# Two kinds of softmax attention in a transformer block kernel: normalising the numerators on GpSimd, and turning them over later

## The reference, cut to what matters

```python
scores = jnp.einsum('bqkgd,bskd->bkgqs', qb, k) * scale
p = jax.nn.softmax(scores, axis=-1)
o = jnp.einsum('bkgqs,bskd->bqkgd', p, v)
y_attn = o * jax.nn.silu(g_a)          # second block only
```

## Time and profile before

| | us |
|---|---|
| median of 3 runs (lowest, highest) | 3885.12 (3881.82, 3887.04) |
| the profiled execution: its time, its span | 3889.09, 3887.3 |
| busy in the span: TensorE, VectorE, ScalarE, GpSimd | 3536.8, 1918.4, 1351.0, 149.0 |
| mean granted TensorE clock | 0.951 of full |
| masked attention, first to last exp | 1330.1 to 1534.7 |
| unmasked attentions, first to last exp | 2790.4 to 2998.5, and one at 3528.7 to 3736.8 |

### The profile page before, as it was taken

The page is one execution under the profiler, slowest core; times in us unless marked ns, Lnnn a source line. Parts: engine busy times, 40 slices in busy tenths (PEclk is TensorE's granted clock), DMA queues, the critical chain, the costliest instruction groups (busy, mean ns, idle before and its releaser), DMA issues.

```text
span 3887.3 us, 41660 instructions
## 1 busy us (share of the span) xinstructions
PE 3536.8 (91%) x17310; PEld 2888.9 (74%) x17310; DVE 1918.4 (49%) x2459; ACT 1351.0 (35%) x1874; POOL 149.0 (4%) x261
## 2 busy tenths in 40 slices
PE   5999999988987698899999998889898988998987
PEld 3888888866975587778888885678887745887875
DVE  6233333366427698353333335622588365137964
ACT  4111111154222388221111113521487064126843
POOL 0000000000100110000000000010100001000000
PEclk8999999999996799999999999999999989999998
DMA  5222221213741453122222221231611103243111
GB/s 194 89 83 71 82 92 66 76 66 98 184 168 39 82 87 61 44 87 71 90 72 78 76 76 38 77 111 60 180 28 33 49 23 102 85 131 98 28 39 44
DMA packets 146619, 316.58 MB, mean 81 GB/s; under 512 B 32616, under 2 KB 96908, under 8 KB 135936
## 3 DMA queue, kind: packets, MB, share of 16 engines
q1 hardware_dynamic: 84880, 216.80, 16.1%
q0 software_dynamic: 61552, 97.12, 10.5%
HBM read 261.79 MB, written 52.09 MB: 81 GB/s over the span
## 4 chain that ended last, share of the span: by engine, by line
PE 79%; DVE 11%; ACT 5%; issue 3%; DMA 1%; POOL 0%; SPq 0%; ACTq 0%; DVEq 0%; POOLq 0%
PE psum L600 56%; PE psum L868 4%; PE psum L891 4%; PE psum L858 4%; PE psum L1015 2%; PE psum L627 2%; PE psum L944 1%; PE psum L698 1%; PE psum L879 1%; DVE h_lo L1495 1%; PE psum L934 1%; ACT attn_th L1283 1%; ACT attn_num L1292 1%; PE psum L792 1%; DVE p_u L1582 0%
## 5 line engine op out<-in xcount | busy, mean ns | idle before, releaser
L600 PE MATMUL psum<-h_hi,w_hi 128*128 128x512 f32 x2112 | 835.0, 395 | 45.0 <-DVE h_lo L1495 26.8
L600 PE MATMUL psum<-h_lo,w_hi 128*128 128x512 f32 x2112 | 826.6, 391 | 0.0
L600 PE MATMUL psum<-h_hi,w_lo 128*128 128x512 f32 x2112 | 826.2, 391 | 0.0
L600 PEld LDWEIGHTS psum<-h_hi,w_hi 128*128 128x128 f32 x2112 | 399.1, 189 | 142.7 <-issue 46.1
L600 PEld LDWEIGHTS psum<-h_lo,w_hi 128*128 128x128 f32 x2112 | 399.4, 189 | 83.1 <-issue 2.9
L600 PEld LDWEIGHTS psum<-h_hi,w_lo 128*128 128x128 f32 x2112 | 399.1, 189 | 83.5
L1051 ACT ACTIVATE w_hi<-w_raw 128x2048 fp32r<-128x2048 f32 (+2 forms) x147 | 249.1, 1695 | 572.1 <-PE psum L600 468.1
L1445 DVE TENSOR_TENSOR w_lo<-w_raw,w_hi 128x2048 fp32r<-128x2048 f32 (+2 forms) x147 | 296.9, 2020 | 262.2 <-ACT w_hi L1051 261.5
L1544 DVE TENSOR_TENSOR gate<-gate,psum 128x1024 f32<-128x1024 f32 x44 | 53.7, 1221 | 608.2 <-PE psum L600 608.2
L600 PE MATMUL psum<-a_hi,w_hi 128*128 128x512 f32 x704 | 274.3, 390 | 3.4 <-DVE a_lo L1546 3.4
L600 PE MATMUL psum<-a_hi,w_lo 128*128 128x512 f32 x704 | 274.1, 389 | 0.0
(11 more groups left out here) (332 smaller groups left out, 5703.5 us busy)
## 6 DMA issues: line engine op xcount, KB each, us to landing
w_raw<-in_w_ada SPq DMA_DIRECT2D x52, 1024.0 KB, 5.0
w_raw<-in_w_gu SPq DMA_DIRECT2D x44, 1024.0 KB, 5.4
w_raw<-in_w_in SPq DMA_DIRECT2D x34, 1024.0 KB, 4.8
w_raw<-in_dft SPq DMA_DIRECT2D x16, 1024.0 KB, 5.2
w_raw<-in_w_down SPq DMA_DIRECT2D x24, 512.0 KB, 3.6
w_raw<-in_w_out SPq DMA_DIRECT2D x12, 1024.0 KB, 5.2
w_raw<-in_w_down SPq DMA_DIRECT2D x16, 640.0 KB, 4.3
qk_hi_scratch<-p_out_hi POOLq DMA_DIRECT2D x18, 512.0 KB, 2.9
```

What stands on the lines that cost most here:

```text
L600: mm = e.matmul(p.half[h], a[:, k * width + m * P:k * width + (m + 1) * P], b(k)[:, h * HALF:(h + 1) * HALF], start=(k == order[0] and i = ...
```

## The change

- GpSimd multiplies each unit's numerators in SBUF by the reciprocal of their sum, in place, before they are turned over. The diagonals (ScalarE), their spread (TensorE) and VectorE's multiplication are gone.
- Numerators and sums lie in rings of three. `turn_over`, `num_high` and `low_parts` of unit u stand in step u + 2 instead of u + 1; `times_v` in the steps after.
- Results are taken for four units (512 queries) at once: one ScalarE copy and one VectorE addition, in step 8 + 4z.
- The rounding at the end of a pair of heads moves from the results' step to steps 22 + 16 pp (ScalarE) and 23 + 16 pp (VectorE) for pair pp, and the unmasked gate's multiplication goes from VectorE to GpSimd.
- The masked attention works with negated scores (negated query gain and band; minimum instead of maximum; exp with scale -1), so that L1827 is gone.
- The mask moves into a weight tile and is loaded by SyncE after the last store before the attention, without waiting for that store; the later weight blocks wait for the last maximum. SyncE loads the gates too; keys and values load at fixed steps; the constant ones are not loaded.

The diff cut to its core:

```diff
-        a.nu = rings(f"{name}_num", 2, [P, S], F32, scope)
+        a.nu = rings(f"{name}_num", 3, [P, S], F32, scope)
...
-        a.tm = [t.sqh[0][0:64, i * 256:(i + 1) * 256] for i in range(2)]
+        a.sm = rings(f"{name}_sm", 3, [P, 4], F32, scope)
+        a.tm = [t.sqh[i][0:64, :] for i in range(2)]
...
+    t.mix1.at.mask = t.raw[first_out1 % RAW][:, 0:1920]
...
             def turn_over(u):
-                e.wait_ge(*exped.at(name, u))
+                e.wait_ge(*num_scaled.at(name, u))
...
             def times_v(w, part):
...
+                    if w % 2 == 0 and z >= 2:
+                        e.wait_ge(*res_done.at(name, z - 2))
...
             for u in range(n + 4):
                 if u < n:
                     scores(u)
-                if 1 <= u <= n:
-                    turn_over(u - 1)
-                if u >= 3 and u % 2 == 1 and u < n + 3:
-                    spread_sum(u - 3)
-                    spread_sum(u - 2)
-                    times_v((u - 3) // 2, 0)
-                if u >= 4 and u % 2 == 0:
-                    times_v((u - 4) // 2, 1)
+                if 2 <= u < n + 2:
+                    turn_over(u - 2)
+                if u >= 4:
+                    times_v((u - 4) // 2, u % 2)
...
+            def half_result(z):
+                e.wait_ge(*pv_done.at(name, 2 * z + 1))
...
+                e.activation(a.tm[z % 2], ps.of[(name, "o")].half[z % 2][64:128, :], ACT.Identity).then_inc(*half_res.mark(name, z))
+
+            def heads_high(pp):
+                e.wait_ge(*(res_done.at(name, 4 * pp + 3) if masked else og_gated.at(name, pp)))
+                e.activation(mixa[0][:, pp, :], a.og[:], ACT.Identity).then_inc(*mix_hi.mark(mix, "a", pp))
...
+            for u in range(n + 8):
+                if 2 <= u < n + 2:
+                    num_high(u - 2)
                 if u < n:
                     numerators(u)
-                if 1 <= u <= n:
-                    diagonal(u - 1)
+                if u >= 8 and u % 4 == 0 and u < n + 8:
+                    half_result((u - 8) // 4)
+                if u >= 22 and (u - 22) % 16 == 0:
+                    heads_high((u - 22) // 16)
...
+            def results(z):
+
+                hh, pp = (z // 2) % 2, z // 4
+                e.wait_ge(*half_res.at(name, z))
+                if z % 4 == 0 and pp:
                     e.wait_ge(*mix_lo.at(mix, "a", pp - 1))
...
+                e.tensor_tensor(a.og[64 * hh:64 * hh + 64, (z % 2) * HALF:(z % 2 + 1) * HALF], ps.of[(name, "o")].half[z % 2][0:64, :],
+                                a.tm[z % 2], ALU.add).then_inc(*res_done.mark(name, z))
...
+            for u in range(n + 8):
                 if u < n:
                     maximum(u)
-                if u >= 5 and u % 2 == 1:
-                    results((u - 5) // 2)
-                if 1 <= u <= n:
-                    low_parts(u - 1)
+                if 1 <= u < n + 1:
+                    s = a.sm[(u - 1) % 3]
                     e.wait_ge(*exped.at(name, u - 1))
-                    e.reciprocal(a.sm[(u - 1) % 2][:, 3:4], a.sm[(u - 1) % 2][:, 2:3]).then_inc(*recip.mark(name, u - 1))
+                    e.reciprocal(s[:, 3:4], s[:, 2:3]).then_inc(*recip.mark(name, u - 1))
+                if 2 <= u < n + 2:
+                    low_parts(u - 2)
+                if u >= 8 and u % 4 == 0 and u < n + 8:
+                    results((u - 8) // 4)
+                if u >= 23 and (u - 23) % 16 == 0:
+                    heads_low((u - 23) // 16)
...
             load_kv(name, a, 1)
...
+            for u in range(n + 8):
+                hd, i = u // ST, u % ST
+                if u < n:
+                    s, m = a.nu[u % 3], a.sm[u % 3]
+                    e.wait_ge(*recip.at(name, u))
+                    e.tensor_scalar(s[:], s[:], m[:, 3:4], None, ALU.mult).then_inc(*num_scaled.mark(name, u))
+                if i == 7 and hd + 2 < A_HEADS:
+                    load_q(name, a, hd + 2)
+                if i in (0, 1) and 1 <= hd < n_kv - 1:
+                    load_k(name, a, hd + 1, i)
+                if i == 3 and 1 <= hd < n_kv - 1:
+                    load_v(name, a, hd + 1)
+                if gated and u >= 20 and (u - 20) % 16 == 0:
+                    pp = (u - 20) // 16
+                    e.wait_ge(*res_done.at(name, 4 * pp + 3))
+                    e.wait_ge(*at_gate.at(name, pp))
+                    e.tensor_tensor(a.og[:], a.og[:], a.g[:], ALU.mult).then_inc(*og_gated.mark(name, pp))
...
         mlstm()
+        e.wait_ge(*w_done.at(first_out1))
+        e.dma_start(t.mix1.at.mask[:], ins["band"]).then_inc(*at_const.mark("attn1"))
+        e.wait_ge(*maxed.at("attn1", A_HEADS * ST - 1))
```

More of the change, by code:

```diff
@@ L497, in program_of @@
     rope_sum, rope_turn, v_turned = (signal(n, "PE") for n in ("rope_sum", "rope_turn", "v_turned"))
-    scored, num_turned, spread, pv_done = (signal(n, "PE") for n in ("scored", "num_turned", "spread", "pv_done"))
+    scored, num_turned, pv_done = (signal(n, "PE") for n in ("scored", "num_turned", "pv_done"))
     ml_pe, four_pe = signal("ml_pe", "PE"), signal("four_pe", "PE")
@@ L564, in program_of @@
             split_at.append(n)
+    first_out1 = next(n for n, entry in enumerate(plan) if entry[3] == ("out1", 0))
+    t.mix1.at.mask = t.raw[first_out1 % RAW][:, 0:1920]
     def place_before(n):
@@ L867, in turn_over @@
                     for j in range(4):
-                        mm = e.transpose(p_t.half[h][:, j * P:(j + 1) * P], a.nu[u % 2][:, (4 * h + j) * P:(4 * h + j + 1) * P],
+                        mm = e.transpose(p_t.half[h][:, j * P:(j + 1) * P], a.nu[u % 3][:, (4 * h + j) * P:(4 * h + j + 1) * P],
                                          ident)
                     mm.then_inc(*num_turned.mark(name, u, h))
[L872 to L881, removed]
             def times_v(w, part):
                 hd, i = (2 * w) // ST, (2 * w) % ST
-                kv = kv_of(hd)
+                kv, z = kv_of(hd), w // 2
                 if part == 0:
@@ L889, in times_v @@
                         e.wait_ge(*v_in[kv % 2].at(name, kv))
+                    if w % 2 == 0 and z >= 2:
+                        e.wait_ge(*res_done.at(name, z - 2))
                 for j in range(ST):
-                    mm = e.matmul(p_o.half[w % 2][:, 0:256], a.v[kv % 2][:, j, :], (a.th, a.tl)[part][w % 2][:, j, :],
-                                  start=(part == 0 and j == 0), stop=(part == 1 and j == ST - 1))
+                    mm = e.matmul(p_o.half[z % 2][:, (w % 2) * 256:(w % 2 + 1) * 256], a.v[kv % 2][:, j, :],
+                                  (a.th, a.tl)[part][w % 2][:, j, :], start=(part == 0 and j == 0),
+                                  stop=(part == 1 and j == ST - 1))
                 if part == 1:
@@ L2223, in gpsimd_program @@
         fence("attn1")
-        for h in (1, 2):
-            e.wait_ge(*st_stored[h % 2].at("ml", h))
-        e.wait_ge(*ml_stored3.at())
-        e.dma_start(t.mix1.at.mask[:], ins["band"]).then_inc(*at_const.mark("attn1", "mask"))
-        attention("attn1", t.mix1.at, A_HEADS, None)
+        ml_drained(e)
+        attention("attn1", t.mix1.at, A_HEADS, False)
         load_mix(t.mix1, "mix1", "attn1", 0)
@@ L2285, in mlstm, with attention_gates @@
             e.dma_start(d.mix[M_HEADS - 1], m.st[1][:]).then_inc(*ml_stored3.mark())
+        def attention_gates(l):
+            name, a = f"attn2_{l}", t.b2[l].at
+            for who in ("PE", "ACT", "DVE"):
+                e.wait_ge(*passed(who, name))
+            e.wait_ge(*fo_stored.at(l))
+            for pp in range(4):
+                if pp:
+                    e.wait_ge(*mix_lo.at(f"mix2{l}", "a", pp - 1))
+                e.dma_start(a.g[:], d.proj[10 + pp]).then_inc(*at_gate.mark(name, pp))
         def fourier(l):
@@ L2289, in fourier @@
             e.wait_ge(*passed("PE", f"fourier{l}"))
-            for j in range(2):
+            for j in (0, 1):
                 e.wait_ge(*st_stored[j % 4].at(f"p2b{l}", j))
@@ L2387, in shape_constants @@
     count = (j <= 64).astype(int) + ((j % 4 == 0) & (j <= 256)) + (j % 16 == 0)
-    band = np.where(count > 0, np.log(np.maximum(count, 1)), NEG).astype(f)
+    band = np.where(count > 0, -np.log(np.maximum(count, 1)), -NEG).astype(f)
     sel = np.zeros((36, 8, P), f)
```

127 lines of the change are left out of this document (44 added, 83 removed).

## The result

| | before | after |
|---|---|---|
| median (lowest, highest), 4 runs of each side by side | 3883.55 (3881.82, 3887.04) | 4051.32 (4050.36, 4052.26) |
| ratio, with its 95% interval | 1 | 1.0431 (1.0413 to 1.0449) |
| span of the profiled execution, granted clock | 3887.3, 0.951 | 4048.6, 0.944 |

A forecast was written before the change was run, and what follows sets the result against it. It took VectorE to bound the masked attention and TensorE to be nearly full unmasked. Masked -12.0 and two unmasked together -26.0 made -38 on 3885.1, so 3847 us; range 3820 to 3897, the forecast's own 3833 to 3862.

The forecast's parts named there:

- d: Time of GpSimd's pass over 128x1024 numerators, taken as 1.2 us, between 0.61 and 2.4.
- Rival A: GpSimd is slow and becomes the bound: 3926 us at d = 2.3, deciding from about 1.9; chance 0.17.
- loop over GpSimd: Scores, maximum, reciprocal, pass, transposes, v products, closing over two units: (4.49 + d) / 2 = 2.85 us unmasked, 2.91 masked.
- VectorE wait in results: Every fourth unit VectorE waits for exp and copy before its addition: 3.06 us a unit masked, 2.95 unmasked.
- The rates: Time from exp to exp inside the attentions: 3.00 us a unit unmasked and 3.08 masked.
- The ends of pairs: Stalls where pairs of heads end, at most 5.1 us unmasked and 3.0 masked, shrink to 0.5 for each of three.
- The start of the masked attention: Mask issued right behind the last store, first maximum about 1324.5 instead of 1328.5: -4 us, between 0 and -7.
- The end of an unmasked attention: Mixer loads stand behind the gate's product on GpSimd: +2 us, 0 to +4 with a long product.
- drain: End of each attention: 1.2 + 0.15 + 0.10 ahead of the last transposes, less 0.35 for the spread: +1.1 us.
- Rival B: Small waits come back, each loop 0.1 us above the rate taken, ends of pairs keep 1: 3866 to 3872; chance 0.13.
- Rival C: ScalarE's copy doesn't hold VectorE, so rates fall to 2.95 masked and 2.85 unmasked: 3820 us; chance 0.12.
- The signs: Profile signs of a wrong forecast: passes above 1.9, transposes released by GpSimd, copy not ahead of addition, clock below full.

The follow-up runs named there:

- two_ops: The changed kernel with a second operation, times 1.0, in GpSimd's pass, which then takes 1.12 us instead of 2.84: 3847.53 us, ratio 0.9909.
- half: The changed kernel with GpSimd's pass over 512 of 1024 columns, the other numerators left unscaled: 3890.34 us, ratio 1.0025.
- copy_first: The changed kernel with ScalarE's copy of the results ahead of its exp in every fourth step: 3988.94 us, ratio 1.0278.
- floor: The changed kernel with GpSimd's pass over only 8 of 1024 columns, the other numerators left unscaled: 3816.32 us, ratio 0.9835.
- lag3: The changed kernel with rings of four and everything from the turning over on one step later: 3863.3 us, ratio 0.9959.
- before_ends: The kernel before with only rounding and remainder at the end of a pair of heads moved a step apart: 3860.5 us, ratio 0.9951.
- two_first: The changed kernel with the times 1.0 operation in GpSimd's pass and ScalarE's copy ahead of its exp: 3816.27 us, ratio 0.9827.

## Why the prediction was wrong, and where it was right

**The step that failed is the price of GpSimd's pass.** The prediction took d = 1.2 between 0.61 and 2.4, from passes of VectorE and ScalarE, since no row showed GpSimd compute. It measured 2.84, above both ends. Twice VectorE's time was no bound at all. The range ended at d = 2.0, so it missed as well. Of the 204 us between forecast and result, 3847.5 for two_ops shows nearly all to be d: with d = 1.12 and nothing else touched, the kernel takes what was forecast, 3847.

The Trainium skill, "GPSIMD Engine Reference", section "Engine selection", calls GpSimd's operations with one input roughly line-rate and those with two about twice as slow. The two-operation form agrees if line-rate means VectorE's 1.22 for a pass over 128x1024 out of PSUM; VectorE's own pass over one tensor in SBUF takes 0.61. The one-operation form does not: 2.84 is 2.3 times the first and 4.7 times the second, with one tensor input. The gate's product with two inputs agrees: 2.35 to 2.38 on GpSimd against VectorE's 1.23.

**Rival A had the right mechanism and the wrong size.** It said loop over GpSimd, transposes released by it; both are in the rows after. But at d = 2.84 its formula gives (4.49 + 2.84) / 2 = 3.67 a unit unmasked, and 4.09 was measured. Its point of decision, 1.9, was too high too. Two things were missing:

- *A second way round the loop.* The prediction counted ScalarE's exp and copy as a wait of VectorE's only. They are also a way from one pass of GpSimd to the next but one: pass and hop d + 0.05, transposes until the high part 0.69, high part until the exp 0.97, exp until the copy 1.23, copy 0.63, addition 0.60, maximum 1.14, reciprocal 0.24, in all 5.55 + d (from 3019.78 on in the changed kernel: 8.40). Of four units, two go this way and two by TensorE, 4.49 + d. The mean is (10.04 + 2d) / 4. The rounds of two_ops show both ways: 5.55 to 5.58 by TensorE, where 5.61 was to be, and 6.69 to 6.84 by ScalarE, where 6.67 was, but 7.8 in the three with the gate's product. At 1.12 the mean is 3.07, measured 3.10; at 1.57 it is 3.29, measured 3.31; so with 3.30 before, the break-even is near d = 1.58, where half's ratio is 1.0025. copy_first takes the exp out of this way, and 62 us go. At d = 0.3 it gives 2.66, less than TensorE's own 2.76, and floor measured 2.95: there another limit holds, such as the prediction's VectorE wait in results. Its 2.95 unmasked would fit, its 3.06 masked does not (floor has 2.94), so this limit stays open.
- *TensorE's clock.* At 2.84 the formula gives 3.93, and 4.09 was measured. Of the unmasked attention's rounds by TensorE, six behind its first steps have a granted clock of 1.00 and take 7.29 to 7.32, as (4.49 + d) says; the nine others have 0.80 to 0.81, in five of them with scores products of 0.63 us, and take 8.55 to 8.87. These nine give up 12.5 us together, 0.20 a unit, enough for the 0.16 that the formula lacks. The rounds by ScalarE have 1.00. TensorE was idle for 2.1 to 2.7 us before the transposes in each of the nine and for 0.9 to 1.4 in four of the six, but for 2.5 and 2.0 in the other two, so idle time of that length goes with the lower clock and does not always bring it. In the stretches of half, two_ops and lag3 the clock was 1.00.

**The rates** were 3.00 and 3.08. With d as assumed, two_ops has 3.10 and 3.08: unmasked 3 us an attention too low (192.0 against 195.1), by the missing way. Masked the number is right (195.5 forecast for the stretch, 194.0 measured), but it came from 3.06 for VectorE's wait in results, and floor, which keeps that wait, runs at 2.94: that wait didn't set it, and another limit, most likely the loop, gave the same number. The unmasked sum for that wait doesn't follow from its own terms either: 1.14 + 1.12 + 0.60 + 0.66 + 0.15 is 3.67 and not 3.77, which makes 2.93 of 2.95 and changes nothing else.

That two_ops as a whole meets the forecast to 1 us owes something to luck. Beside its own runs of the kernel before it is 35 us faster, where 38 was forecast. By the spans (3843.3 against 3887.3) it is 44; 6.3 of these lie ahead of the last store before the attention (1310.0 against 1316.3), where the work is the same and kernels of this form had 1309.6 to 1316.1. The exps of its attentions give 10.6 + 2 x 13.0 = 36.6, where 41.3 was forecast, and the rest between them 1.1, where 3.3 more was forecast: two misses that cancel.

**The ends of pairs** were right in kind: before_ends gains 20 us by moving the rounding alone. The prediction's stalls would have given up to 3 x (3.0 - 0.5) + 6 x (5.1 - 0.5) = 35 at the most.

**The start of the masked attention** was put at -4 and came out at 8.39 instead of 12.26 from the store to the first maximum, -3.9. It lay between the ends of the range: the mask took 7.9 us from issue to landing instead of 4.9. The keys and values were issued at 1320.18, 5.9 us behind the mask, so the store beside it is the likelier cause; no run separates the two.

**The end of an unmasked attention** was put at +2 with a drain of +1.1. The idle time before the loaded tiles grew by 2.7 (8.21 against 5.47), with the gate's 2.35 in it, as the long product's end of the range had it; the drain grew by 3.5 (last exp to first product of the projection, 10.31 against 6.85), with the longer pass in it; in two_ops it grew by the 1.1 that was forecast (7.96). Behind the second attention most of this was made up before the third began (its stretch grew by 1.1 only), for a reason not looked into; behind the third it stayed, +6.9.

**Rival B,** small waits that come back, has its number in two_ops unmasked, 0.1 above the rate taken, but not its cause: that is one missing way round the loop, not many small waits. **Rival C,** that the copy wouldn't hold VectorE, is refuted by copy_first and two_first: moving the copy is worth 62 us at d = 2.84 and 31 at 1.12.

**The signs** named ahead were the right ones: passes above 1.9, transposes released by GpSimd, and a granted clock below full all came.

## What to carry to other kernels

When work moves to an engine whose price no row shows, the neighbours' prices are no bound. Measure that very form of instruction first: here an added "times 1.0" took the pass from 2.84 to 1.12 us and made a loss of 4.3% a gain of 0.9%. When a long operation is put between engines, draw every way round from it back to itself, those through the queue order of a third engine too; if none of the engines is full, a unit more of lag (188 us here) or two statements in another order (62 us) can be worth a good part of what the faster pass is (204 us here).

## What the runs showed of the hardware

- GpSimd's one-operation tensor_scalar over f32 takes 0.29 us and 2.49 ns a column, the same for 64 and 128 partitions. Over 128x1024 it takes 2.84, with a constant 2.77. With two operations it takes 1.12, a copy 1.035, tensor_tensor with a broadcast second operand 1.89, with two full inputs 2.35 to 2.44.
- VectorE and GpSimd can hold one another up in SBUF. VectorE's tensor_scalar above took 0.33 us in the median and up to 2.29. In lag3, with GpSimd busy 98%, VectorE's remainder with two inputs in SBUF took 2.18 in the median instead of 1.22; where it took 1.24, at 2954.53, the pass that GpSimd had begun at the same moment took 3.88 instead of 2.84:

```profile
L1836 DVE TENSOR_TENSOR mix2a_lo<-attn_o,mix2a_hi x8: 1225/2176/2190, 2853.2 to 3716.4; 128x1024 fp32r<-128x1024 f32 x8
```

In two_ops the same line has 1.22 in the median. By the Trainium skill, "SBUF — State Buffer", section "Who interferes with whom", the two share a pair of ports as an exclusive lock, taken by VectorE's two-port forms, tensor_scalar among them, and in part by its instructions with two SBUF inputs. The rows above agree. But seven of the 192 small passes of VectorE lay wholly inside a pass of GpSimd and took 0.32 to 0.34 all the same, which such a lock does not explain. ScalarE, which the same section leaves out of it, did the 256 columns in 0.49 to 0.56.
- The granted clock over 52 us of the changed attention was 0.90. Nine rounds of one attention with TensorE idle for 2.1 to 2.7 us had 0.80 to 0.81, and in five of the nine scores products took 0.63 instead of 0.40 us; two rounds with 2.0 and 2.5 us of idle time kept 1.00.
